# Three chained transformer blocks on one core: norms with one ScalarE table set and weighted squares, a new order of the first loads, and one wait in the expert loop moved

## The reference

```python
def rmsnorm(x, g):
    xf = x.astype(jnp.float32)
    y = xf * lax.rsqrt(jnp.mean(xf * xf, axis=-1, keepdims=True) + NORM_EPS)
    return (y * g.astype(jnp.float32)).astype(x.dtype)
```

## Time and profile before

| | |
|---|---|
| median of 3 executions | 2894.58 us (2890.18 to 2898.1) |
| the profiled execution | 2892.35 us, span 2890.6 us |
| TensorE busy | 2760.3 us, 95% of the span |
| ScalarE, VectorE busy | 1207.2 us, 1416.6 us |
| chain that ended last | PE 89%, ACT 4%, DVE 3%, DMA 2% |
| expert loop | about 381 to 1361 us, 12 of 40 slices at 422 GB/s |
| mean granted TensorE clock | 0.984 |

### The profile page before, as it was taken

The page is one execution under the profiler, slowest core; times in us unless marked ns, Lnnn a source line. Parts: engine busy times, 40 slices in busy tenths (PEclk is TensorE's granted clock), DMA queues, the critical chain, the costliest instruction groups (busy, mean ns, idle before and its releaser), DMA issues.

```text
span 2890.6 us, 54886 instructions
## 1 busy us (share of the span) xinstructions
PE 2760.3 (95%) x21288; PEld 2215.2 (77%) x21288; DVE 1416.6 (49%) x2958; ACT 1207.2 (42%) x2129; POOL 73.5 (3%) x140
## 2 busy tenths in 40 slices
PE   6999999999999999999989999999999999998997
PEld 5779865555656565655878989999998888888997
DVE  2545522122222222222346548887657777666773
ACT  3434422222222222222245454467775455555772
POOL 0000000000000000000000000000001000000000
PEclk9999989999999999999999999999999999999998
DMA  5775789999999999999375546655557777533452
GB/s 243 276 281 201 273 333 422 422 422 422 422 422 422 422 422 422 422 422 377 124 300 204 190 157 222 217 185 179 169 173 254 240 238 244 207 118 116 161 189 89
DMA packets 114937, 796.61 MB, mean 276 GB/s; under 512 B 13680, under 2 KB 13680, under 8 KB 22128
## 3 DMA queue, kind: packets, MB, share of 16 engines
q1 hardware_dynamic: 103536, 753.97, 67.2%
q0 software_dynamic: 11264, 40.71, 4.0%
HBM read 776.54 MB, written 18.09 MB: 275 GB/s over the span
## 4 chain that ended last, share of the span: by engine, by line
PE 89%; ACT 4%; DVE 3%; DMA 2%; issue 1%; POOL 0%; DVEq 0%; ACTq 0%; SPq 0%; POOLq 0%
PE psum L1028 16%; PE psum L784 15%; PE psum L1382 12%; PE psum L1348 11%; PE psum L1057 8%; PE psum L986 4%; PE psum L996 2%; PE psum L654 2%; PE psum L1474 2%; PE psum L1367 2%; PE psum L1007 2%; PE psum L800 1%; PE psum L711 1%; DMA weight_ring<-in_stream 1%; ACT work L2569 1%
## 5 line engine op out<-in xcount | busy, mean ns | idle before, releaser
L1929 DVE TENSOR_TENSOR work<-psum,work 128x256 f32<-128x256 f32 x132 | 56.1, 425 | 718.9 <-PE psum L1007 718.9
L1608 DVE TENSOR_TENSOR ring_parts<-weight_ring,peer_parts 128x1024 fp32r<-128x1024 f32 x218 | 262.4, 1223 | 260.8 <-ACT peer_parts L2618 214.3
L2618 ACT ACTIVATE peer_parts<-weight_ring 128x1024 fp32r<-128x1024 f32 x218 | 225.1, 1054 | 267.9 <-PE psum L784 130.6
L1382 PE MATMUL psum<-v_high,h_low 128*128 128x512 f32 x1024 | 253.0, 389 | 2.9 <-ACT v_high L2961 2.9
L1028 PE MATMUL psum<-weight_ring,work 128*64 128x256 f32 x2112 | 243.4, 383 | 0.8 <-ACT work L2754 0.8
L1057 PE MATMUL psum<-work 128*64 128x512 f32 x1056 | 233.9, 595 | 0.0
L1382 PEld LDWEIGHTS psum<-v_high,h_low 128*128 128x128 f32 x1024 | 192.1, 188 | 42.9 <-issue 3.0
L1028 PEld LDWEIGHTS psum<-weight_ring,work 128*64 128x64 f32 x2112 | 149.8, 138 | 92.8 <-issue 26.8
L2261 DVE TENSOR_TENSOR ring_parts<-weight_ring,peer_parts 128x1024 fp32r<-128x1024 f32 x128 | 156.8, 1225 | 102.2 <-ACT peer_parts L2917 101.9
L2961 ACT ACTIVATE v_high<-weight_ring 128x1024 fp32r<-128x1024 f32 x128 | 135.8, 1061 | 169.8 <-PE psum L1382 169.8
L2417 DVE TENSOR_TENSOR ring_parts<-weight_ring,v_high 128x1024 fp32r<-128x1024 f32 x128 | 156.9, 1226 | 78.1 <-ACT v_high L2961 78.1
(11 more groups left out here) (320 smaller groups left out, 4736.4 us busy)
## 6 DMA issues: line engine op xcount, KB each, us to landing
weight_ring<-in_stream SPq DMA_DIRECT2D x455, 1024.0 KB, 5.4
work<-in_stream SPq DMA_DIRECT2D x198, 1024.0 KB, 14.1
chunkbuf<-in_stream SPq DMA_DIRECT2D x66, 1024.0 KB, 14.4
peer_scores<-chunkbuf POOLq DMA_DIRECT2D x61, 256.0 KB, 5.4
chunkbuf<-peer_scores POOLq DMA_DIRECT2D x61, 256.0 KB, 2.9
work<-in_rows POOLq DMA_DIRECT2D x1, 1312.0 KB, 16.9
xT<-in_x POOLq DMA_DIRECT2D x1, 1024.0 KB, 10.5
work<-in_ctx POOLq DMA_DIRECT2D x1, 1024.0 KB, 18.8
```

Of the source, the lines that this page charges most:

```text
L1382: mm = pe.matmul(psum[:, 2 * t + h, :], wt[:, t * P:(t + 1) * P], v[:, h * 512:(h + 1) * 512], start=(first and k == 0), stop=False, skip_ ...
L1608: ve.tensor_tensor(split[s].at(ring_parts, q), split[s].at(ring, q), high_halves[:, q % HIGHS, :].bitcast(F32), ALU.subtract).then_inc(spl ...
L2618: sc.activation(high_halves[:, q % HIGHS, :], split[s].at(ring, q), ACT.Copy).then_inc(split[s].high, 1)
```

## The change

1. **Weighted squares.** The squares for the second norm are taken with the root of g^2 + eps as scale, so their sum alone gives the joint root; VectorE's `under_roots` and the second half of the joint Ln and Exp go. The plain squares come after them, are added partly after the first product of the next block (4 + 4 chunks, then 5 + 3), and get a root of their own (`rs:o1`, `rs:o2`); `gained_next` moves behind it. The roots of the gains are made by `gains_of_next` after the attention of block 1.
2. **One table set.** `preload_act_table_set(LN_EXP)` loads a set with both Ln and Exp at seven places, before the wait that follows.
3. **`unread`** becomes shorter or goes (12, 14, 22, 26, 20, 26 to 5, 0, 0, 0, 0, 10; 6 new before the last norm).
4. **Splits of weights move.** `highs(24)` and `highs(16)` stand between the squares, `lows` of the same piece inside the residual; `highs(12)` and the squares of the attention come before those of the convolution in block 3, and each branch gets its root by itself; `highs(0)` and `lows(0)` of block 3 move ahead of the squares and of the last copy of block 2.
5. **First loads.** SP asks for the vectors, the identity and x, then the ring. POOL asks for context and `rows` when the eighth piece of `ada1` has landed. TensorE multiplies all eight pieces, then k1x, the sum of the context's squares, v1x, k1c, v1c.
6. **Experts.** `turned(3)` stands after the first down piece.

```diff
-                unread("o1", E, 14)
-                mean_squares(1, E)
-                unread("x2", E, 22)
+                mean_square_next(1, E)
+                mean_square_out(1, E, 0, 4)
...
                 columns("kc", 0, hT, "x2")
+                mean_square_out(1, E, 4, DC)
...
-                    pe.wait_ge(nar_g, e * 4 + 4)
-                    pe.wait_ge(nar_b, e * 4 + 3)
-                    turned(3)
                     pe.wait_ge(nar_xe, e + 2)
                     for k in range(4):
+                        if k == 1:
+                            pe.wait_ge(nar_g, e * 4 + 4)
+                            pe.wait_ge(nar_b, e * 4 + 3)
+                            turned(3)
...
-                conditioning(1, 0, 4, True)
-                mean_square("ctx", E, m["merged"], DC)
-                conditioning(1, 4, 8)
+                conditioning(1, 0, 8, True)
...
-                unread("mixed3", E, 20)
...
-                mean_square("o3", E, m["sq"], DC)
+                unread("o3", E, 6, 5)
+                mean_square("o3", E, m["sq"], DC, 4)
...
+            sp.dma_start(vec[:, :], dram["vec"]).then_inc(x_in, 16)
+            sp.dma_start(ident[:, :], dram["ident"]).then_inc(x_in, 16)
+            sp.dma_start(xT[:, :, :], dram["x"]).then_inc(x_in, 16)
...
-            gp.dma_start(xT[:, :, :], dram["x"]).then_inc(x_in, 16)
-            gp.dma_start(vec[:, :], dram["vec"]).then_inc(x_in, 16)
-            gp.dma_start(ident[:, :], dram["ident"]).then_inc(x_in, 16)
+                gp.wait_ge(*landed(first_piece["ada1"] + 7))
+                gp.dma_start(m["ctxT"], dram["ctx"]).then_inc(tables_in[1], 16)
                 gp.dma_start(m["rows"], dram["rows1"]).then_inc(tables_in[1], 16)
-                gp.dma_start(m["ctxT"], dram["ctx"]).then_inc(tables_in[1], 16)
```

```diff
                 attention(1, 16, A_, m)
+                gains_of_next(A_)
                 sc.wait_ge(*at("mod1a"))
                 row("mod1b", 0, "ada2:7", 0, A_)
                 highs(4, 1)
...
                 for k in (2, 3, 4):
                     lows(k, 2)
+                gained_next(1, V)
                 ve.wait_ge(*at("kcmp"))
...
                     v_low(p)
+                lows(0)
                 ve.wait_ge(*at("peer_y"))
                 ve.tensor_copy(m["y_nat"][:, 1, 0:512], psum[:, 2, :]).then_inc(...)
                 residual_sum(2, "y_turned", V, mod_cols(2, 5))
-                under_roots(2, V)
...
-                squares_twice(2, A_)
+                sc.preload_act_table_set(LN_EXP)
                 highs(0)
-                two_roots(2, A_)
+                squares_next(2, A_)
+                inverse_root("x3", A_, roots[2], eps_squared[2])
```

More of the change, by code:

```diff
@@ L1792, in residual @@
                                                 ALU.mult, ALU.add).then_inc(*V.up(*names))
+                    if i == 2 and next_low is not None:
+                        lows(next_low, s)
             def residual_sum(s, tag, V, gate):
@@ L2574, in row, with squares @@
                 act(A_, mod_rows[:, k, :], psum[:, 7, at0:at0 + 256], ACT.Copy, f"row:{tag}", *names)
-            def squares(tag, A_, src, sq, chunks, ready):
-                for i in range(chunks // 2):
+            def squares(tag, A_, src, sq, chunks, ready, first=0):
+                for i in range(first, chunks // 2):
                     if ready:
@@ L2592, in two_roots @@
[L2592 to L2604 removed]
+                        act(A_, A[s]["sq"][:, c, :], xT[:, c, :], ACT.Square,
+                            *([f"sq:x{s + 1}:{i}"] if c % 2 else []), scale=gain_roots[s][:, c:c + 1])
@@ new lines, in squares_next, with gains_of_next, inverse_root @@
+                for i in range(DC // 2):
+                    act(A_, sq_next[s][:, 2 * i:2 * i + 2, :], xT[:, 2 * i:2 * i + 2, :], ACT.Square, f"sq:o{s}:{i}")
+            def gains_of_next(A_):
+                for s, roots_of in gain_roots.items():
+                    sc.wait_ge(*at(f"gains_squared:{s}"))
+                    act(A_, roots_of, roots_of, ACT.Ln)
+                    sc.wait_ge(*A_.now())
+                    act(A_, roots_of, roots_of, ACT.Exp, scale=0.5)
+            def inverse_root(tag, A_, dst, bias, chunks=DC):
+                sc.wait_ge(*at(f"ms:{tag}"))
+                act(A_, dst, bank_of(f"ms:{tag}")[:, 0:T], ACT.Ln, f"free:ms:{tag}", scale=D / (P * chunks), bias=bias)
+                sc.wait_ge(*A_.now())
+                act(A_, dst, dst, ACT.Exp, f"rs:{tag}", scale=-0.5)
@@ L2606, in shifted, with root @@
+            def root(tag, A_, m, chunks=DC, rs="rs"):
+                inverse_root(tag, A_, m[rs], m["v"]["eps"], chunks)
             def shifted(tag, A_, sq, dst, gain, shift, gains):
@@ L2631, in shifted_parts, with mixed_highs @@
                             scale=gain[:, c:c + 1], bias=shift[:, c:c + 1])
-            def mixed_highs(m, A_, at0):
-                for c in range(at0, at0 + 4):
+            def mixed_highs(m, A_, first, last):
+                for c in range(first, last):
                     sc.wait_ge(*at(f"h:mixed3:{c}"))
```

177 lines of the change are left out of this document (85 added, 92 removed).

## The result

| | before | changed |
|---|---|---|
| median | 2894.58 us (2890.18 to 2898.10, 5 runs) | 2876.76 us (2872.38 to 2881.81, 5 runs) |
| ratio of the times | | 0.9939, 95% interval 0.9922 to 0.9957 |
| profiled execution | 2892.35 us, span 2890.6 | 2874.15 us, span 2872.3 |
| TensorE busy | 2760.3 us | 2746.0 us |

A forecast was written before the change was run, and what follows sets the result against it. The prediction took TensorE, busy 95% of the span, as the bound, with memory traffic at 422 GB/s limiting the expert loop. Terms summed to -30.8 us: 2861.5 against the profiled execution, plus 2.2 for the median, 2864; range 2850 to 2876.

The forecast's parts named there:

- Expert loop: Moving turned(3) hides a 0.72 us wait per item, but the last load's slack limits the gain: -4.4 us.
- Start: Earlier first loads; context and rows land by 43, then 3.7 for their sum and 21.2 for three products: -4.5 us.
- Gains: After block 1's attention, gains_of_next ahead of highs(4) on ScalarE makes TensorE's product wait: +3.0 us.
- Block 1 to 2: Passage between blocks: weighted squares first, 16 products and one root, Exp 10 us earlier, 1.8 given back: -8.0 us.
- product-key norm: Norm before the product-key layer: one pair of high parts between the squares and no table load: -4.3 us.
- output product: Block 3: the attention's squares and highs(12) move into ScalarE's idle time, each root goes by itself: -5.6 us.
- last norm: Final norm: sum at full clock, banks freed in order, one load fewer: -6.3 us, or -3.2 at half clock.
- rival of the lower clock at the passages: Shorter unread leaves TensorE at 1.2 GHz after passages and norms, about 3 us each: 2873 to 2879; chance 0.07.
- Block 2 to 3: Passage between blocks: lows(0) waits for highs(0) and delays the fourth copy, so TensorE waits 6 us: +3.7 us net.
- The loop is not bound by memory: Rival, expert loop: the queue can exceed 422 GB/s, so turned(3) brings all 23.7 us: 2845; chance, wholly or partly, 0.08.
- Stalls of a loop bound by memory bring the clock down: Rival, expert loop: load waits cause half clock, items take 32.1 us, kernel 2922; chance of slower 0.03.
- A switch costs more than its load: Rival, ScalarE table loads: activations behind a load start late, so ten removed loads save another 13 us: 2851; chance 0.02.

The follow-up runs named there:

- before_loop_both: The kernel before, with only turned(3) after the first down piece and ScalarE's copy of the next item's inputs ahead of the last hidden quarter: 2891.18 us, ratio 0.9985.
- parts_as_before: The changed kernel with block 3's lows(0) back behind the residual and highs(0) behind the squares: 2873.47 us, ratio 0.9924 to the kernel before.
- loop_both: The changed kernel with ScalarE's copy of the next item's expert inputs moved ahead of the last hidden quarter: 2872.71 us, ratio 0.9926 to the kernel before.
- high_first: The changed kernel with block 3's highs(0) ahead of ScalarE's three copies of the layer's result: 2874.15 us, ratio 0.9925 to the kernel before.

## Why the prediction was wrong

- **Expert loop, -4.4 forecast, +2.1 measured: the step that failed** is "`turned(3)` behind the first down piece hides the 0.72 us". In its place the first down product waited 0.60 us for ScalarE's copy, 19.2 us over the loop, and the item grew from 29.39 to 29.45. The limit of the loads behind it is real (items of 29.8 us in before_loop_both, a loop 3.2 us shorter where 4.4 were forecast), but the change never reached it, since that second wait was hidden under the one that it removed. The row of ScalarE's copy, ending 0.02 us before VectorE's bias in the trace before the change, could have been read there. That a loop bound by loads also pays 2.3 us at the branch behind it had no place in the forecast.
- **Start, -4.5 forecast, -1.0 measured.** x landed at 8.83, not near 6.5; the sum then held the first slot for 4 us more; and "they land at 41 to 43" was 45.57, which counts in full, since the context's squares wait for both loads. The step "43 + 3.7 + 21.2" named the right chain with a start that was too early.
- **Gains, +3.0 forecast: right** as to the wait, 2.9. That TensorE falls to half clock behind a wait of 3.13 us cost 2.1 more, which the sum did not have.
- **Block 1 to 2, product-key norm, output product, feed-forward norm, last norm** came within 0.4 us each, and so did the experts' norm with its one table load. The rival of the lower clock at the passages did not come true as a whole: the last sum took 3.69 us, at full clock, the sum at block 1 to 2 ran partly at half clock, as the forecast allowed.
- **Block 2 to 3, +3.7 forecast, +3.5 measured**, by the chain forecast. parts_as_before shows that the order cost 4.2: without it this passage would have been 0.7 faster than before.
- **Short stretches of half clock** (102, 334, 364 to 384, 1557 and 2163 us) stood in one of the two profiles and not in the other, or were of another length; they had no place in the forecast, and the last section shows one. Apart from the 2.1 behind the gains, which the wait there caused, the parts with a forecast of 0 come to +0.6 in sum, and that it is so little is luck.
- **Rivals.** "The loop is not bound by memory" is refuted by the 29.82 us items of loop_both. "Stalls of a loop bound by memory bring the clock down" is refuted by the same windows: 1.00 in both. "A switch costs more than its load" found no row for it.
- **The sum.** The terms add up to -30.9, not -30.8, which changes nothing.
- In sum: of the 12.6 us that are missing, 6.5 are the second wait in the loop, 3.5 the start and 2.1 the half clock behind the gains.

## What to carry to other kernels

Before a wait is priced at its full length, look at what else the waiting engine needs next and when each of those was ready: a wait shows only the last of them, and one that ended 0.02 us earlier took its place here. In a loop fed by loads, compare bytes per item over the measured rate with the item's time, and read the landing times at both ends: what could be gained here was the slack of the last load less 1.0 us, however many waits were taken away. Of loads asked for in one go, give each the semaphore of its first reader.

## What was not expected of the hardware

The same product runs at full or at half clock in different executions of kernels that are equal up to there. Windows of 1556 to 1562 us in the changed kernel, and then in high_first, whose first edit comes 950 us later:

```profile
1556.00:1562.00 6.00, 6.00 (x56) 5.88 (x54) 5.74 (x15) 2.01 (x2) 0.00 (x0) 1.00 0.44 180
```

```profile
1556.00:1562.00 6.00, 6.00 (x32) 5.78 (x29) 5.79 (x15) 2.00 (x2) 0.00 (x0) 0.50 0.36 153
```

TensorE is busy all the time in both, and in the six us ahead of them; the granted clock is 1.00 in one and 0.50 in the other, and 3.0 us are lost. Of the seventeen profiles seven have a stretch of 3.4 or 6.8 us at half clock at this place, that of the kernel before among them, and ten have none. Some four or five places of the program behave so (102, 334, 1557, 2583 us among them), which by their size can account for the 9 us between a kernel's fastest and slowest run; that they do was not tested. It is also why a single profile tells local gains by the distance between two instructions, and not by the span.
